# A one-layer attention and expert kernel: projection pieces in halves, two gate groups and the norm inputs moved

## The reference

```python
u = x * (1 + sc1) + sh1
xc, bg, cg, q, k, v, g_conv, g_na = jnp.split(u @ w_in, IN_SPLITS, axis=-1)
y_conv = short_conv(xc, bg, cg, conv_w)                 # bg * conv3(cg * xc)
y_na = neighbourhood_attention(q, k, v, k_ctx, v_ctx, rpb)   # latent; softmax attention for the context
merged = (jax.nn.sigmoid(g_conv) * (y_conv @ w_conv_out) +
          jax.nn.sigmoid(g_na) * (y_na @ w_na_out))
x = layer_norm(ALPHA * x + ga1 * (merged @ w_o), ln1_g, ln1_b)
u2 = x * (1 + sc2) + sh2
x = layer_norm(ALPHA * x + ga2 * peer(u2, w_query, sub_keys, expert_u, expert_v), ln2_g, ln2_b)
```

## Time and profile before

| what | value |
|---|---|
| median of three runs | 1862.25 us |
| profiled execution, its own time | 1859.29 us |
| its span, first to last instruction | 1857.5 us |
| mean granted clock of TensorE | 0.986 |
| PE busy | 1766.8 us, 95% |
| DVE busy | 1267.7 us, 68% |
| POOL busy | 903.7 us, 49% |
| ACT busy | 298.4 us, 16% |
| bytes moved by DMA | 670.16 MB, 361 GB/s over the span |

### The profile page before, as it was taken

One profiled execution on the slowest core, in us unless ns is written; L12 is line 12 of the kernel. 1 busy time (PEld: TensorE's weight loads), 2 busy tenths in 40 slices (PEclk: granted clock), 3 DMA queues, 4 the chain that ended last, 5 costly groups with the idle time before them and its releaser, 6 DMA issues.

```text
span 1857.5 us, 20549 instructions
## 1 busy us (share of the span) xinstructions
PE 1766.8 (95%) x7508; PEld 1103.8 (59%) x7508; DVE 1267.7 (68%) x2592; ACT 298.4 (16%) x689; POOL 903.7 (49%) x818
## 2 busy tenths in 40 slices
PE   5987999998999999999999999999899999999996
PEld 3675844554444458678888888886554434444442
DVE  1212568989579799989999888869855323336767
ACT  0120012555000001111100100116630000000000
POOL 1000336656456323356675666567765554435541
PEclk9998999998999999999999999999999999999998
DMA  9997769888999968779999999999999999999995
GB/s 395 394 362 301 287 197 395 313 316 308 384 339 406 397 241 324 249 263 409 395 409 405 409 397 408 399 398 355 361 363 410 409 343 409 409 410 409 409 410 234
DMA packets 171205, 670.16 MB, mean 361 GB/s; under 512 B 19770, under 2 KB 20922, under 8 KB 166364
## 3 DMA queue, kind: packets, MB, share of 16 engines
q0 software_dynamic: 112368, 409.74, 57.8%
q1 hardware_dynamic: 53984, 243.29, 33.5%
q10 hardware_dynamic: 4752, 15.81, 2.2%
HBM read 659.27 MB, written 7.39 MB: 359 GB/s over the span
## 4 chain that ended last, share of the span: by engine, by line
PE 43%; DVE 24%; DMA 17%; POOL 8%; issue 6%; ACT 1%; SPq 1%; DVEq 0%; ACTq 0%; POOLq 0%
PE psum L1057 18%; DMA arena<-in_expert_u_dram,arena 8%; POOL arena L641 8%; DVE psum L1991 7%; DMA arena<-in_expert_v_dram,arena 6%; DVE arena L1700 5%; PE psum L840 3%; PE psum L829 3%; PE psum L1010 2%; PE psum L815 2%; PE psum L1081 2%; PE psum L1084 2%; PE psum L1118 2%; PE psum L1178 2%; PE psum L826 1%
## 5 line engine op out<-in xcount | busy, mean ns | idle before, releaser
L641 POOL DMA_INDIRECT arena<-in_expert_u_dram,arena x384 | 484.2, 1261 | 314.1 <-DVE arena L1700 187.3
L641 POOL DMA_INDIRECT arena<-in_expert_v_dram,arena x384 | 384.4, 1001 | 365.5 <-DVE psum L1991 187.0
L1700 DVE CUSTOM_DVE_ANT_0 arena<-arena 128x1024 f32<-128x1024 f32 x384 | 458.5, 1222 | 137.4 <-DMA arena<-in_expert_u_dram,arena 136.1
L1991 DVE SCALAR_TENSOR_TENSOR psum<-arena,psum 128x1024 f32<-128x1024 f32 x254 | 327.1, 1288 | 198.0 <-DMA arena<-in_expert_v_dram,arena 183.9
L1057 PE MATMUL psum<-arena 128*128 128x512 f32 x1024 | 442.9, 594 | 0.8 <-DMA arena<-in_expert_v_dram 0.8
L983 PE MATMUL psum<-arena 128*128 128x256 f32 x2048 | 442.7, 379 | 0.0
L983 PEld LDWEIGHTS psum<-arena 128*128 128x128 f32 x2048 | 389.2, 190 | 52.3
L1057 PEld LDWEIGHTS psum<-arena 128*128 128x128 f32 x1024 | 193.7, 190 | 250.1 <-issue 249.9
L1478 ACT ACTIVATE arena<-psum 128x512 f32<-128x512 f32 x64 | 38.2, 597 | 373.2 <-PE psum L983 373.2
L840 PE MATMUL psum<-arena 128*128 128x512 f32 x192 | 86.9, 605 | 0.8 <-ACT arena L1264 0.8
L1155 PE MATMUL psum<-arena 128*128 128x384 f32 x256 | 85.2, 486 | 0.0
(11 more groups left out here) (201 smaller groups left out, 1490.2 us busy)
## 6 DMA issues: line engine op xcount, KB each, us to landing
arena<-in_expert_uT_dram SPq DMA_DIRECT2D x128, 512.0 KB, 6.8
arena<-in_expert_v_dram SPq DMA_DIRECT2D x128, 512.0 KB, 6.8
arena<-in_w_ada_dram SPq DMA_DIRECT2D x12, 2048.0 KB, 13.7
arena<-in_w_in_dram SPq DMA_DIRECT2D x11, 2048.0 KB, 12.4
arena<-in_w_query_dram SPq DMA_DIRECT2D x8, 2048.0 KB, 11.3
arena<-in_w_in_dram SPq DMA_DIRECT2D x30, 512.0 KB, 8.4
arena<-in_w_o_dram SPq DMA_DIRECT2D x16, 512.0 KB, 6.7
arena<-in_expert_u_dram,arena POOLq DMA_INDIRECT x384, 9.8
```

The costliest lines, as they stand in the source:

```text
L641: pool.indirect_dma_start(slot, None, table[0], bass.IndirectOffsetOnAxis(ap=number, axis=0)).then_inc(land, 16)
L1700: dve.tensor_tensor_reduce(row, row, U2B[e], 1.0, 0.0, ALU.mult, ALU.add, DOTS[e % 2][:, k:k + 1]).then_inc(u_free, 1)
L1991: dve.scalar_tensor_tensor(ys, row, weight, ys, ALU.mult, ALU.add).then_inc(v_free, 1)
```

## The change

It has five parts.

1. **Halves.** The third of every three pieces of the projection is cut into two halves of four matmuls (`project_half`), one in the third iteration and one in the fourth, which had none. `PIECE_AFTER` is worked out from the new table `HALVES` and tells ACT after which iteration a piece is complete.
2. **Gates inside the loop's end.** The convolution's gates of d = 8 are computed in halves in iterations 14 and 15 (`first_gate`, bank 5), those of d = 9 in iteration 16 (`second_gate`, bank 0). The merge's first step then computes attention's gates of d = 8 and 9 at once (banks 1 and 4) and its branches; the second has its branches only. ACT takes two sigmoids of 128x512 for each of the two.
3. **Rows.** `PAIR_ROWS` has 62 rows instead of 70, and the convolution's part on DVE comes ahead of a pair's last rows; `BEFORE_MERGE` is 22 instead of 12; the first two steps of the merge take 7 rows each instead of 8.
4. **Norm inputs.** The five broadcasts of the latent norm are issued after the sigmoid of d = 12 (`ROWS_STEP`). The gelu of tile 0 comes after the sigmoid of d = 10 instead of d = 9.
5. **Groups.** `SCORED_GROUPS` is 10: 80 rows of tile 2 are scored ahead of the gates instead of 88, and 48 behind them instead of 40.

The diff, cut to its core:

```diff
-PIECE_AFTER = {0: 1, 1: 2, 2: 3, 4: 4, 5: 5, 6: 6, 8: 7, 9: 8, 10: 9, 12: 10, 13: 11}
+HALVES = (2, 2, 1, 1, 2, 2, 1, 1, 2, 2, 1, 1, 2, 2)
+HALVES_TO = [2 + sum(HALVES[:i]) for i in range(len(HALVES) + 1)]
+PIECE_AFTER = {i: [m for m in range(1, 12) if HALVES_TO[i] <= 2 * m + 1 < HALVES_TO[i + 1]] for i in range(len(HALVES))}
+GATE_HALVES, GATE_NEXT = {14: 0, 15: 1}, 16
+GATE_BANKS = {8: (5, 1), 9: (0, 4)}
...
+            def first_gate(half):
+                wc = merge_weights(pe, "gconv", 1, 0, 0)
+                if half == 0:
+                    pe.wait_ge(proj_out, PROJ_QKV + 12)
+                for k in range(4 * half, 4 * half + 4):
+                    pe.matmul(bank(5), wc[:, k, :], UT[:, k, CTX:NT], start=k == 0, stop=k == KD - 1)
+            def second_gate():
+                wc = merge_weights(pe, "gconv", 1, 0, 1)
+                pe.wait_ge(win_step, NU - 2)
                 for k in range(KD):
+                    pe.matmul(bank(0), wc[:, k, :], UT[:, k, CTX:NT], start=k == 0, stop=k == KD - 1)
...
-                    if i in PIECE_AFTER:
-                        project_piece(PIECE_AFTER[i])
+                    if i < len(HALVES):
+                        for half in range(HALVES_TO[i], HALVES_TO[i + 1]):
+                            project_half(half)
+                    if i in GATE_HALVES:
+                        first_gate(GATE_HALVES[i])
+                    if i == GATE_NEXT:
+                        second_gate()
...
+                    if s == 1 and i == ROWS_STEP:
+                        load_rows(s)
...
-                    context_rows(rows - 2)
                     if i in CONV_AFTER:
                         convolve_piece(CONV_AFTER[i])
+                    context_rows(max(rows - 2, 0))
...
-SCORED_GROUPS, GATE_ROUNDS = 11, 20
+SCORED_GROUPS, GATE_ROUNDS = 10, 20
...
-PAIR_ROWS = (6, 6, 4, 2, 6, 6, 4, 2, 6, 6, 4, 2, 6, 6, 2, 2)
-BEFORE_MERGE = 12
-MERGE_ROWS, NORM_ROWS = (8, 8, 14, 14, 14, 14, 12, 3), 4
+PAIR_ROWS = (6, 6, 1, 3, 6, 6, 1, 3, 6, 6, 1, 3, 6, 6, 1, 1)
+BEFORE_MERGE = 22
+MERGE_ROWS, NORM_ROWS = (7, 7, 14, 14, 14, 14, 12, 3), 4
+ROWS_STEP = 4
```

More of the change, by code:

```diff
@@ L956, in latent_attention @@
             def latent_attention():
-                project_piece(0)
+                project_half(0)
+                project_half(1)
                 for i, n in enumerate(range(2, NU + 4, 2)):
@@ L1351, in latent_attention @@
                         take_out(n - 3)
-                    if i in PIECE_AFTER:
-                        take_piece(PIECE_AFTER[i])
+                    for m in PIECE_AFTER.get(i, ()):
+                        take_piece(m)
             def normalise(n):
@@ L1364, in load_x, with load_rows @@
                 act.dma_start(XB[min(e, 1)], rows(x_prompt, x_sample, e)).then_inc(xb_in, 16)
+            def load_rows(s):
+                own = mods_d[s:s + 1, :]
+                for n, row in ((0, own[:, 2 * D:3 * D]), (1, ln1_g[0:1, :]), (2, ln1_b[0:1, :]),
+                               (3, own[:, 4 * D:5 * D]), (4, own[:, 3 * D:4 * D])):
+                    act.dma_start(PRM[s][n], row.partition_broadcast(P)).then_inc(prm_in[s], 16)
             def section(s):
@@ L1369, in section @@
                     act.wait_ge(mods_out, 16)
-                else:
-                    act.wait_ge(win_step, NU - 2)
-                own = mods_d[s:s + 1, :]
-                for n, row in ((0, own[:, 2 * D:3 * D]), (1, ln1_g[0:1, :]), (2, ln1_b[0:1, :]),
-                               (3, own[:, 4 * D:5 * D]), (4, own[:, 3 * D:4 * D])):
-                    act.dma_start(PRM[s][n], row.partition_broadcast(P)).then_inc(prm_in[s], 16)
+                    load_rows(s)
                 for i in range(8):
```

44 lines of the change are left out of this document (28 added, 16 removed).

## The result

The changed kernel takes 1869.21 us (median of 20 runs) where the kernel before takes 1863.7 in 20 runs: a ratio of 1.0034 over all runs, 95% interval 1.0021 to 1.0046. It is slower, by some 6 us, and outside the range that was forecast. Its profiled execution has a span of 1870.3 us against 1857.5. These two executions lie 12.8 us apart, the medians only 5.5: the one before was 4.4 us faster than its median, the one after 2.9 slower. So what follows from this pair of profiles shows where time goes, and is larger than the usual difference.

The account below looks back on a forecast made before the run. PE was taken to bound the kernel, with DMA as second resource. Terms -11.5 - 6.4 + 5 + 4 + 0.5 = -8.4 take 1859.29 us to 1850.9, forecast as a 1853.9 us median; range 1844 to 1865.

Parts of the forecast that it names:

- A, the loop: Latent attention's loop: half pieces cover the turn-around if DVE follows with fewer rows; -11.5 us, bounds 13.3 and 6 gained.
- Rival 2: Loop of latent attention: DVE sets the pace and half of the loop's gain is lost, 1859.7 us; chance 0.12.
- B, the loop's end: End of the attention loop: with two gate groups added it takes 24.5 us instead of 19.54, +5.0 us.
- B, the wait between the branches: Second merge step: its branches wait for DVE's multiplication and two handovers, 1.4 to 3.7 us, taken as 2.5.
- rival 3: Ahead of the first merge: slow POOL issues starve DVE's 22 rows, first merge 9.4 us late, 1865.1 us; chance 0.12.
- the fast one: POOL issue at 459.72 in the earlier trace: took 0.94 us while DVE scored, so the slow-issue rule agreed in part only.
- C, the broadcasts: Later merge: five broadcasts, 2.62 MB, keep DVE's rows from being fetched and delay the output projection; +5 us, bounds 0 and 6.5.
- The count of bytes: From 441.42 to 628.87 us: 74.4 MB at 406 GB/s need 183.3 us of 187.45, allowing at most 4.2 us of gain.
- D, the end: Dense sum's end: eight more rows behind the gates, partly absorbed by POOL's pause; +4 us, bounds 0 and 8.
- Rival 4: Dense sum: POOL's pause moves with the rows instead of shrinking, so value rows end late, 1869.2 us; chance 0.14.
- The summand rounds and the middle: Behind the scored rows: summand rounds reach PE later, 0.5 us of wait, up to 3.

Follow-up runs that it names:

- e6: The kernel before with only the projection's halves; gates, rows, norm inputs and groups as before: ratio 0.9987 to the kernel before.
- e4: The changed kernel with 11 groups of tile 2 scored ahead of the gates, as before: ratio 1.0020 to the kernel before.
- e13: The changed kernel with the tokens for the 36 rows behind the loop read from a PSUM copy: ratio 1.0016 to the kernel before.
- e1: The changed kernel with the query weights' loads also waiting for DVE's last merge: ratio 0.9981 to the kernel before.
- e3: The changed kernel with the broadcasts issued behind DVE's last merge and the query weights behind them: ratio 0.9962 to the kernel before.
- e14: The changed kernel with broadcasts last, 14 and 15 rows around the first merge, 11 groups, tokens in PSUM: ratio 0.9933 to the kernel before.
- e16: The changed kernel with broadcasts last, 11 groups, tokens in PSUM, its own 22, 7 and 7 rows: ratio 0.9914 to the kernel before.
- e2: The changed kernel with the five broadcasts back at the end of latent attention: ratio 0.9994 to the kernel before.

## Why the prediction was wrong

Step by step, from the profiled executions of both kernels:

- **A, the loop: right in size, half right in reason.** Forecast -11.5; measured 126.11 - 138.65 = -12.5. But the reason given, that half a piece covers the turn-around of 6.1 us, is not enough: e6 shows 0.5 us for halves alone. DVE's rows had to go too, which the step counted as a condition. Rival 2's mechanism was there in the kernel before, and the change's new rows took it away. And the step took all 13.3 us for waiting: by its own row PE idled 6.89 of them, and the other 6.4 were its slower clock. That the clock rose to 1.00 as well made the size right; this part was luck.
- **B, the loop's end: right.** Forecast +5.0, measured 23.95 - 19.54 = +4.4 at full clock.
- **B, the wait between the branches: the first term that failed.** "2.5, the middle" priced two handovers and DVE's multiplication. Measured 7.58 of wait and 6.26 - 3.60 = 2.66 of slower clock, 10.2 us; in e4, the same code to this point, 4.21 and 2.60. DVE was not there to multiply: rival 3, which had 0.12. Its mechanism was right in kind: the fourteen issues from 444.08 on take 1.43 us in the mean, with 0.30 between them 1.73, where 1.60 was the limit, and the first merge was 6.3 us late. Its 11.2 came close by luck: it had the merge 9.4 late and nothing for the clock. Part of the lateness is not POOL's: DMA moves 365 GB/s from 457 us on and 402 from 470, where 406 is what the prediction called full. The sign was at hand in the kernel before, one and two issues behind the fast one that outweighed it:

```profile
460.96 1.97 POOL L641 DMA_INDIRECT arena<-in_expert_u_dram,arena  x1 [0.31 <-issue]
463.24 1.99 POOL L641 DMA_INDIRECT arena<-in_expert_u_dram,arena  x1 [0.30 <-issue]
```

With the two of the earlier trace rows, three of four issues beside DVE's scoring are slow, and the four take 2.02 us in the mean with the gap. The Trainium skill's rule in "SBUF — State Buffer", section "Who interferes with whom", is about a VectorE instruction with two SBUF inputs and a GpSimd instruction that reads SBUF. e13 agrees with it if an issue counts as such an instruction, which the rule itself does not say.
- **C, the broadcasts: the second term that failed, in what it left out.** Forecast +5, bounds 0 and 6.5; measured 18.87 - 2.85 = +16.0. The broadcasts themselves are 5.9 of it (e1 to e3), inside the bounds. Another 8.8 are the query loads (e1): a DVE that is late for its last merge is a thing PE doesn't wait for until the merge's end, and PE's branches released 4.2 MB into the gap. The step asked what falls among the rows because it was moved; it did not ask what else is released by the engine that gets ahead. The Trainium skill says that each DMA engine goes round between the queue rows that have work ("DMA: Bandwidth & Descriptors", section "Queues, rings and completion order"). The 4.12 and 4.87 us agree with it in so far as rows of POOL's queue came late while loads of SP's moved; no run shows the turns themselves.
- **The count of bytes proved little.** It had 74.4 MB (with eight more rows, where step A takes only six out of the loop); the query loads' 4.2 MB were not in it, and it can't see a stretch of 245 GB/s in which POOL is the limit.
- **D, the end: right.** Forecast +4; measured from -3.0 to +1.4, +4.3. Its mechanism held: from 1460 to 1513 us DMA moves 409 GB/s where it was 351, and POOL's longest wait for a sum of PE is 9.8 us instead of 19.60. Only the bound of 0, "PE's end still covers it", was not open, since the end follows DVE's last row in the kernel before too. Rival 4 gave 1869.2, almost the time measured, by a mechanism that did not happen: D kept its size.
- **The summand rounds and the middle:** 0.5 forecast, 0.3 measured (from the projection's start to PE's end 1211.1 us against 1210.8).

The sum is -12.5 + 4.4 - 13.9 + 10.2 + 16.0 + 4.3 + 0.3 = +8.8; the span grew by 12.8. The rest is the loop's start, 306.37 against 302.77, in code that the change doesn't touch: in the study's seventeen other profiles it lies between 299.9 and 306.3. What in front of the loop makes it differ stays open. For the size of the other terms e4 is a second sample of the same code up to the projection: from the loop's start to there it takes 326.5 us, where the changed kernel's profile has 330.7 and the kernel before 326.1. So in one execution the gains and the losses up to the projection cancel, in the other the losses win by 4.6; in both, B's wait and C's loads took back what A and B had gained.

## What to carry to other kernels

When one engine is to get ahead of another, list every load that the leading engine releases: those behind its last step arrive early and take bandwidth from the work that the lagging engine still owes. Before counting rows per stretch, look at what an issue costs beside the very instruction that will run next to it; here an operand's place (SBUF or PSUM) set how fast another engine could issue its DMAs. And a gain on the engine that looks idle is worth what the engine that feeds it can follow: test the parts alone, and split what they bring into idle time and clock, since here neither the halves (6.51 us of idle time left of 6.89) nor the rows (5.14) brought by themselves what both did (0.25).

## What was not expected of the hardware

- An indirect DMA's issue on POOL takes 0.94 us beside a DVE that adds or waits, and up to 1.99 beside one that scores with two SBUF inputs, though not every time. With one input in PSUM (e13, e14, e16) it is 0.93 or 0.94 every time behind the loop, at the same 1.22 us for DVE.
- After waits of 3.24 to 16.48 us between the branch groups PE ran part of the next four matmuls at 1.2 GHz, and the loss did not grow with the wait: 6.65 us after a wait of 3.24 (e13), 6.20 after 4.21 (e4), 6.26 after 7.58, 5.56 after 16.48 (e2), and 3.67 after 1.43, where 3.60 is usual. The shorter wait of e13 gave nothing of this loss back.
